# Inverse roots of the norms on ScalarE: Exp(-0.5 Ln(v)) in place of Sqrt and a VectorE reciprocal, in a two-layer trunk

## The reference

```python
def rmsnorm(x, g):
    y = x32 * lax.rsqrt(jnp.mean(x32 * x32, axis=-1, keepdims=True) + EPS)
    return (y * g.astype(jnp.float32)).astype(x.dtype)
...
    h = rmsnorm(x, g_norm) @ w_in
    qa, ka, va, qb, kb, vb = jnp.split(...)
    o_sb = stick_breaking(rmsnorm(heads(qa), q_norm_sb), rmsnorm(heads(ka), k_norm_sb), heads(va))
    qb = apply_rope(rmsnorm(heads(qb), q_norm_dil), cos, sin)
    kb = apply_rope(rmsnorm(heads(kb), k_norm_dil), cos, sin)
    o_dil = dilated_attention(qb, kb, heads(vb))
    o = jnp.concatenate([rmsnorm(o_sb, g_out_sb), rmsnorm(o_dil, g_out_dil)], axis=-1)
    return x + o @ w_out
```

## Time and profile before

| | us |
|---|---|
| three runs | 1954.22, 1956.68, 1956.3 |
| median | 1956.3 |
| profiled execution, device time | 1956.61 |
| its span, first to last instruction | 1954.9 |
| TensorE busy in the span | 1918.1 (98%) |
| ScalarE busy | 1187.3 (61%) |
| VectorE busy | 1353.2 (69%) |
| mean granted TensorE clock | 0.993 |

### The profile page before, as it was taken

The page is one execution under the profiler, slowest core; times in us unless marked ns, Lnnn a source line. Parts: engine busy times, 40 slices in busy tenths (PEclk is TensorE's granted clock), DMA queues, the critical chain, the costliest instruction groups (busy, mean ns, idle before and its releaser), DMA issues.

```text
span 1954.9 us, 27154 instructions
## 1 busy us (share of the span) xinstructions
PE 1918.1 (98%) x9152; PEld 1602.2 (82%) x9152; DVE 1353.2 (69%) x1604; ACT 1187.3 (61%) x1501; POOL 140.8 (7%) x152
## 2 busy tenths in 40 slices
PE   9989999999999999999998998999999999999998
PEld 7778888888888888888887887888888888888887
DVE  8766654554544554445567677888989898988996
ACT  7656543443433343334557566787878788787885
POOL 8300000000000000000200001010100010000001
PEclk9999999999999999999999998999999999999999
DMA  9544566666666666666664558999999999999997
GB/s 353 159 139 149 176 192 187 191 193 187 189 194 186 192 185 194 190 190 184 186 183 131 159 173 319 371 395 379 396 373 393 381 393 378 401 379 395 376 395 257
DMA packets 141588, 510.31 MB, mean 261 GB/s; under 512 B 15936, under 2 KB 15952, under 8 KB 140080
## 3 DMA queue, kind: packets, MB, share of 16 engines
q1 hardware_dynamic: 134288, 486.64, 71.5%
q0 software_dynamic: 7200, 22.39, 4.4%
HBM read 495.33 MB, written 13.64 MB: 260 GB/s over the span
## 4 chain that ended last, share of the span: by engine, by line
PE 88%; DMA 3%; ACT 3%; DVE 3%; POOL 2%; issue 1%; POOLq 0%; DVEq 0%; SPq 0%; ACTq 0%
PE main L594 28%; PE main L596 28%; PE main L595 28%; DMA raw_pieces<-in_ffn_moe 3%; DVE w_low L1356 1%; ACT w_high L1023 1%; PE transpose L922 1%; PE transpose L962 1%; PE transpose L612 1%; PE transpose L793 0%; PE transpose L905 0%; DVE heads_scratch L1404 0%; DVE small L1405 0%; PE spread L656 0%; PE transpose L634 0%
## 5 line engine op out<-in xcount | busy, mean ns | idle before, releaser
L1356 DVE TENSOR_TENSOR w_low<-raw_pieces,w_high 128x1024 fp32r<-128x1024 f32 x919 | 1096.6, 1223 | 435.2 <-ACT w_high L1023 428.9
L1023 ACT ACTIVATE w_high<-raw_pieces 128x1024 fp32r<-128x1024 f32 x919 | 949.3, 1058 | 262.4 <-DMA raw_pieces<-in_ffn_dense 125.3
L594 PE MATMUL main<-w_high,xT_high 128*128 128x512 f32 (+1 forms) x1920 | 732.4, 381 | 1.1 <-DVE x_resid L1554 0.7
L596 PE MATMUL main<-w_high,xT_low 128*128 128x512 f32 (+1 forms) x1920 | 722.6, 376 | 0.0
L595 PE MATMUL main<-w_low,xT_high 128*128 128x512 f32 (+1 forms) x1920 | 721.7, 376 | 0.0
L596 PEld LDWEIGHTS main<-w_high,xT_low 128*128 128x128 f32 x1920 | 362.2, 189 | 66.5
L594 PEld LDWEIGHTS main<-w_high,xT_high 128*128 128x128 f32 x1920 | 362.7, 189 | 64.9 <-issue 2.5
L595 PEld LDWEIGHTS main<-w_low,xT_high 128*128 128x128 f32 x1920 | 362.7, 189 | 63.0
L594 PE MATMUL main<-w_high,hT_high 128*128 128x512 f32 x832 | 329.0, 395 | 0.0
L596 PE MATMUL main<-w_high,hT_low 128*128 128x512 f32 x832 | 324.6, 390 | 0.0
L595 PE MATMUL main<-w_low,hT_high 128*128 128x512 f32 x832 | 324.2, 390 | 0.0
(11 more groups left out here) (237 smaller groups left out, 859.5 us busy)
## 6 DMA issues: line engine op xcount, KB each, us to landing
raw_pieces<-in_ffn_moe SPq DMA_DIRECT2D x528, 512.0 KB, 6.0
raw_pieces<-in_ffn_dense SPq DMA_DIRECT2D x264, 512.0 KB, 3.6
raw_pieces<-in_w_in SPq DMA_DIRECT2D x96, 512.0 KB, 3.7
raw_pieces<-in_w_out SPq DMA_DIRECT2D x32, 512.0 KB, 3.6
x_resid<-in_x SPq DMA_DIRECT2D x4, 512.0 KB, 14.7
xn_rows<-token_major POOLq DMA_DIRECT2D x2, 1024.0 KB, 5.2
out_x<-x_resid POOLq DMA_DIRECT2D x4, 512.0 KB, 4.5
token_major<-in_x_t SPq DMA_DIRECT2D x1, 1024.0 KB, 9.8
```

What stands on the lines that cost most here:

```text
L594: pe.matmul(out_ap, lh[ls], rh[rs], start=first, stop=False)
L596: return pe.matmul(out_ap, ll[ls], rh[rs], start=False, stop=last)
L1023: act.activation(WH[:, piece % RING, :], RAWS[:, piece % RING, :], ACT.Copy).then_inc(high_done, 1)
L1356: dve.tensor_tensor(WL[:, piece % RING, :], RAWS[:, piece % RING, :], WH[:, piece % RING, :], ALU.subtract).then_inc(low_done, 1)
```

## The change

Each root and reciprocal pair becomes two activations on ScalarE, Ln and then Exp with scale -0.5, the second waiting for the first (`inverse_roots`). The 16 reciprocals on VectorE go; VectorE waits for the root's semaphore where it took them. The roots for x signal `rstd_done` from ScalarE itself and count their mean squares on a semaphore of their own. Every Ln and Exp of a mixer is in one set, which the kernel loads once a mixer: in the first at i = 13 (it was 18), behind the sines; in the second at i = 2 (it was 18).

```diff
@@
-V_OT_SB, V_MS_SB, V_INV_SB = 46, 46, 48
-V_OT_DIL, V_MS_DIL, V_INV_DIL = 53, 55, 57
+V_OT_SB, V_MS_SB, V_ROOT_SB = 46, 46, 48
+V_OT_DIL, V_MS_DIL, V_ROOT_DIL = 53, 55, 57
...
+            def inverse_roots(which, done):
+
+                link(act.activation(which, which, ACT.Ln))
+                act.activation(which, which, ACT.Exp, scale=-0.5).then_inc(done, 1)
+
+            def x_root(norm):
+                act.wait_ge(xms_done, norm + 1)
+                inverse_roots(RSTD[norm], rstd_done)
+
             def roots(which, n):
                 act.wait_ge(ms_done, n + 1)
-                act.activation(which, which, ACT.Sqrt).then_inc(root_done, 1)
+                inverse_roots(which, root_done)
...
-                    act.preload_act_table_set("sqrt_and_others")
+                    act.preload_act_table_set("natural_log_exp_and_others")
...
                     if i == (8 if layer == 0 else T_ROOT):
-                        roots(RSTD[2 * layer], r0)
-                    if i == 18:
+                        x_root(2 * layer)
+                    if i == (13 if layer == 0 else T_ROOT - 1):
                         act.preload_act_table_set("natural_log_exp_and_others")
...
-            def inverse(dst, n):
-
-                dve.wait_ge(root_done, n + 1)
-                return dve.reciprocal(dst, dst)
...
                 def heads_scaled(n, tiles):
                     c, rs = IN_ORDER[n], HSSR[:, 8 * n:8 * n + 8]
                     if 0 in tiles:
-                        link(inverse(rs, r0 + 1 + n))
+                        dve.wait_ge(root_done, r0 + n + 1)
```

More of the change, by code:

```diff
@@ L49 @@
 WARM = 28
-ROOTS = 8
+ROOTS = 6
 GAINS = 2 * KD + 2 * HEADS + 2
@@ L74 @@
 V_SMAX, V_W = {39 + 2 * h: h for h in range(HEADS)}, {41 + 2 * h: h for h in range(HEADS)}
-V_OT_SB, V_MS_SB, V_INV_SB = 46, 46, 48
-V_OT_DIL, V_MS_DIL, V_INV_DIL = 53, 55, 57
+V_OT_SB, V_MS_SB, V_ROOT_SB = 46, 46, 48
+V_OT_DIL, V_MS_DIL, V_ROOT_DIL = 53, 55, 57
 V_ADD_SB, V_ADD_DIL = {50 + 2 * d: d for d in range(DBLOCKS)}, {58: 0, 60: 1, 62: 2}
 V_XT = {60: 0, 62: 1}
-T_ADD, T_SQ, T_PE, T_HIGH, T_LOW, T_MS, T_ROOT, T_INV = 0, 1, 1, 2, 2, 2, 3, 4
+T_ADD, T_SQ, T_PE, T_HIGH, T_LOW, T_MS, T_ROOT = 0, 1, 1, 2, 2, 2, 3
 GU_BLOCKS = 6
@@ L357, in trunk @@
         xg_done = sem("xg_done")
-        ms_done = sem("mean_square_done")
+        ms_done, xms_done = sem("mean_square_done"), sem("x_mean_square_done")
         root_done = sem("root_done")
@@ L1175, in mixer @@
                     if i in A_ROOT:
-                        roots(HSSR[:, 8 * A_ROOT[i]:8 * A_ROOT[i] + 8], r0 + 1 + A_ROOT[i])
+                        roots(HSSR[:, 8 * A_ROOT[i]:8 * A_ROOT[i] + 8], r0 + A_ROOT[i])
                     if i in A_O_SB:
@@ L1187, in mixer @@
                     if i == A_ROOT_SB:
-                        roots(O_RSTD[:, 0:TILES], r0 + 5)
+                        roots(O_RSTD[:, 0:TILES], r0 + 4)
                     if i == A_O_DIL:
@@ L1205, in mixer @@
                     if i == A_ROOT_DIL:
-                        roots(O_RSTD[:, TILES:2 * TILES], r0 + 6)
+                        roots(O_RSTD[:, TILES:2 * TILES], r0 + 5)
                     if i in A_SQ_X:
@@ L1230, in ffn_slice @@
                         if i == T_ROOT:
-                            roots(RSTD[1], ROOTS - 1)
+                            x_root(1)
                     if i in ends:
@@ L1265, in _ @@
             x_high(1, G_FFN, f["tp_x"], 7)
-            roots(RSTD[3], 2 * ROOTS - 1)
+            x_root(3)
             act.wait_ge(rstd_done, 4)
@@ L1357, in low, with mean_squares @@
                                   ALU.subtract).then_inc(low_done, 1)
-            def mean_squares(dst, sums, count):
-                dve.tensor_scalar(dst, sums, 1.0 / count, EPS, ALU.mult, ALU.add).then_inc(ms_done, 1)
-            def inverse(dst, n):
-                dve.wait_ge(root_done, n + 1)
-                return dve.reciprocal(dst, dst)
+            def mean_squares(dst, sums, count, done=ms_done):
+                dve.tensor_scalar(dst, sums, 1.0 / count, EPS, ALU.mult, ALU.add).then_inc(done, 1)
             def x_mean_squares(norm):
@@ L1371, in x_mean_squares @@
                 link(dve.tensor_reduce(SS, SSP[:, :].rearrange("p (t d) -> p t d", t=TILES), AX.X, ALU.add))
-                mean_squares(RSTD[norm], SS, D)
-            def x_inverse(norm):
-                inverse(RSTD[norm], ROOTS * (norm // 2) + (ROOTS - 1) * (norm % 2)).then_inc(rstd_done, 1)
+                mean_squares(RSTD[norm], SS, D, xms_done)
             def turned_low(high, dst, chunk, gains, n):
@@ L1529, in mixer @@
                         mean_squares(O_RSTD[:, 0:TILES], O_SS[:, 0:TILES], HEADS * DH)
-                    if i == V_INV_SB:
-                        link(inverse(O_RSTD[:, 0:TILES], r0 + 5))
+                    if i == V_ROOT_SB:
+                        dve.wait_ge(root_done, r0 + 5)
                     if i in V_ADD_SB:
@@ L1538, in mixer @@
                         mean_squares(O_RSTD[:, TILES:2 * TILES], O_SS[:, TILES:2 * TILES], HEADS * DH)
-                    if i == V_INV_DIL:
-                        link(inverse(O_RSTD[:, TILES:2 * TILES], r0 + 6))
+                    if i == V_ROOT_DIL:
+                        dve.wait_ge(root_done, r0 + 6)
                     if i in V_ADD_DIL:
```

6 lines of the change are left out of this document (removed).

## The result

| | us | runs |
|---|---|---|
| before, median (range) | 1955.87 (1953.37 to 1956.68) | 6 |
| change, median (range) | 1945.24 (1944.69 to 1948.85) | 6 |
| change over before | 0.9942 [0.9931, 0.9953] | |
| profiled execution, device time | 1944.98 | 1 |
| its span | 1943.0 | 1 |

The change is faster, by 10.6 us between the medians, which is 0.6%. The forecast was 12.0 us, its range 1941 to 1949.

A forecast was written before the change was run, and what follows sets the result against it. TensorE, busy 98% of the span, bounds the kernel, so only its waits count. Head 2 -4.0, head 3 -5.4, clock behind head 3 -5.4, moved load +1.1, clock at L634 +1.7: -12.0, to 1944.3 us; range 1941 to 1949.

The forecast's parts named there:

- Head 2: Suffix sums (L656): three table loads go, the whole 2.03 us wait goes; 2.0 per mixer, 4.0 in all.
- Head 3: Suffix sums (L656): two table loads go, the 3.99 us wait falls to about 1.3; 2.7 per mixer, 5.4 in all.
- The clock behind head 3: TensorE after head 3's suffix sums: the fall to 1.2 GHz no longer happens; 2.7 per mixer, 5.4 in all.
- The moved load: First mixer, behind the sines: the load delays the second block's squares, so the wait at L634 grows by 1.1 us.
- the pair of activations cancel against the reciprocal: Chain before L634: the extra activation's 0.23 us on ScalarE offsets the removed reciprocal's 0.23 on VectorE.
- The clock at L634: First mixer's turned heads: a wait of about 3.4 us may lower the clock; 0.65 of 2.7 gives +1.7.
- What was priced at nothing: Routing (L865), and loads moved to attention output norms, x norms and routing exponentials: no cost, TensorE does not wait there.
- Six loads, no reciprocal: Sign in the profile: six table loads in all, 21 fewer, and no reciprocal at L1366.
- a wait at a place without a row: Sign of a wrong prediction: TensorE waits somewhere that the prediction's profile rows do not list.
- the clock stays low: Rival, behind head 3: waits of 1.3 us still cost the low clock, the 5.4 is not had; 1949.7, chance 0.10.
- VectorE is the bound: Rival, suffix sums: VectorE takes back what ScalarE frees, only head 2's idle 1.67 us goes; 1954.1, chance 0.05.
- the slower case: Rival, L634: moved load costs 3.8 with the clock's fall, removed loads were hidden behind VectorE; 1960.1, chance 0.03.

The follow-up runs named there:

- the one-load experiment: The change with one table load put back in head 3's chain, between Exp and Ln, another where ScalarE waits anyway; 1950.09 us, ratio 0.9964.
- load17: Also the first experiment: the change with the first mixer's table load at i = 17, not 13, in a gap of ScalarE; 1941.69 us, ratio 0.9923.
- change_again: The change run once more, unaltered, in the second group of runs on another chip; 1944.75 us, ratio 0.9938 to the kernel before.
- head2_three: The change with three table loads put back around head 2's Exp and Ln and head 1's exponential; 1949.48 us, ratio 0.9967.
- head3_two: The change with two table loads put back in head 3, ahead of its Exp and of its Ln; 1951.98 us, ratio 0.9979.
- log_terms_first: The change with the load at i = 17 and `log_terms` of heads 1 and 3 ahead of the squares; 1947.7 us, ratio 0.9954.
- sines_late: The last experiment: load17 with `log_terms(1)` ahead of the squares and the sines moved from column 12 to 16; 1936.37 us, ratio 0.99.

## Why the prediction was right

*Head 2, forecast 2.0 per mixer.* Its wait is gone in both mixers, and so is VectorE's idle time. Right; putting the loads back restored 2.05 and 2.04.

*Head 3, forecast 2.7 per mixer and 1.3 left.* 1.29 and 1.28 are left. Right, and the loads put back one at a time show the price: 1.29 for the first, 2.56 for both. The Trainium skill, "ScalarE: Activation LUTs", section "What ACT_TABLE_LOAD costs", states a further 1380 ns of drain per switch; by that, two loads would have added 5.3 us, an estimate. In the trace above the activation starts 1.30 us after its load starts (109.25 to 110.55), and the next load starts 0.02 us after that activation ends, so the measurement decides: a load on the chain costs its 1.28.

*The clock behind head 3, forecast 2.7 per mixer.* Right in both traces (2.69 each), yet less firm than it read. The fall behind such a wait cost 2.7 in the profile of before and 1.6 where the loads were put back, with 6.8 and 3.4 us of low clock. I had one execution and took its size for fixed.

*The moved load, forecast +1.1.* Near: 14.85 - 13.62 = 1.23. I had let the pair of activations cancel against the reciprocal; it costs 0.22 more on this chain, because VectorE's next low part now waits 0.34 us for the high part behind the pair, which starts later.

*The clock at L634, forecast +1.7.* The size of the wait was off as a fixed number, 3.4, since GpSimd, ScalarE and TensorE arrive at other times in each execution: 2.87 and 1.22 in the two profiles of the change, 4.11 with late angles. The rule by which I priced it, in proportion to the distance between a wait without and one with a fall, is the step that does not hold (its own ratio is 0.66, which would give 1.8). The fall comes or does not: the change's profiles show none, the one-load experiment, with the change's own instructions up to there, the whole 1.6. The average came out about right nonetheless, and that is luck: hiding the load gave 3.0 us by the medians, across two chips, against 1.1 + 1.7.

*What was priced at nothing.* L865 kept 3.6 us. From the first product of the experts (L905) to the end of the span it is 774.4 us before and 775.5 after. The nine experiments, eight of them with the change's code there, spread from 772.7 to 775.8; so no cost is shown. Six loads, no reciprocal, as said. One sign of being wrong did come up, a wait at a place without a row: the 1.85 us ahead of the first main product. The forecast had no term for it, and it is not the change's: with the same code there it is 0.25 in load17 and 0.21 in the one-load experiment.

*The rivals.* That the clock stays low did not happen. That VectorE is the bound is excluded by head 2 and head 3 themselves, and the mechanism of the slower case exists, but is 3 us against the 14.8 that the heads give.

*The sum.* The spans of the two profiled executions are 11.9 us apart. From the first L634 to head 3's suffix sums it is 4.7 us less in each mixer, from there on 2.7 less in each, 14.7 in all. Up to the first L634 it is 1.65 more, behind L905 1.1 more, in the dense part 0.1 more. So -11.9 comes near the forecast of -12.0 partly by luck: the +1.7 for the clock at L634 is not in it, and the 1.1 behind L905, where nothing was priced, lies within the spread of 772.7 to 775.8 that executions show there. The medians give -10.6; where the other 1.3 go is open, and the runs of either kernel range over 3 to 4 us.

## What to carry to other kernels

A table load costs its 1.28 us only where it stands on the chain that the matmuls wait for: find the chain first, and either place the load in a gap or choose functions that share a set. Both gave the same here once the shared set's one load was itself in a gap (0.9925 and 0.9923); with it on a chain, as in the change, the shared set gave less (0.9942). Where a change moves a load (or any setup step) ahead of work that was already late, look for a gap on the same engine, and for the instruction in front that waits for a slow engine: here 3.7 us came with moving the sines by four columns. Waits of 2.05 to 2.8 us cost the clock in three of twelve cases here, so removing such a wait can be worth 1.6 us more than its length.

## What the runs showed that I had not expected

*GpSimd at two paces.* The same chain of instructions ends early or late from one execution to the next. Its mask (L485) and last angle (L470) in the profile of the change and in that of the first experiment:

```profile
26.55 1.56 POOL L485 TENSOR_SCALAR neg_union<-branch_count 128x384 f32<-128x384 f32 x1
...
43.90 0.30 POOL L470 TENSOR_SCALAR heads_scratch<-heads_scratch 128x128 f32<-128x128 f32 x1
```

```profile
28.27 2.36 POOL L485 TENSOR_SCALAR neg_union<-branch_count 128x384 f32<-128x384 f32 x1
...
48.44 1.15 POOL L470 TENSOR_SCALAR heads_scratch<-heads_scratch 128x128 f32<-128x128 f32 x1
```

Of eleven profiles six (change, change_again, head2_three, head3_two, log_terms_first, sines_late) have the mask at 1.56 or 1.57 us and the angle at 43.9 to 45.0, five (before among them) 2.36 and 48.2 to 48.8, with nothing between. TensorE's start goes with it: where GpSimd is early, the wait ahead of the first main product is 1.0 to 2.2 us and TensorE comes to the first L634 at 61.3 to 61.7; where it is late, the wait is 0.2 to 1.0 and TensorE comes at 60.5 to 60.7. Before was traced only with late angles and the change only with early ones, so a difference between their two profiles up to the first L634 is not all the change's. What sets the pace is open. By its order the kernel of the last experiment should no longer depend on the angles; no late execution of it was traced.

*The clock does not always fall behind a middling wait.* Over the same profiles, counting the waits at the suffix sums and at L634: of twelve waits of 2.0 to 2.9 us three were followed by the low clock (2.05, 2.58 and 2.80), each at a cost of 1.6 us; all seven of 3.66 to 4.11 were, at 1.6 to 2.8; none of 1.3 or less was. Waits of 2.04 and 2.05 in one execution went either way, and the shortest behind which it fell is 2.05, while it held behind 2.87. Behind L865, with its 3.6, the clock was low for 10.2 us in all eleven, before and after alike.
